# Two fused transformer blocks on one core: the second block's output projection, norms, router logits and last norm with tokens on the partitions

## The reference

```python
h = layer_norm(x) * (1 + sc_m) + sh_m
mix = hybrid_mixer(h, ...)            # ends with  merged @ w_out   (1024 x 1024)
x = layer_norm(alpha * x + g_m * mix, ln_mix_g, ln_mix_b)
h = layer_norm(x) * (1 + sc_f) + sh_f
ffn = grouped_moe(h, ...)             # h @ w_router, top 2 of 16 experts, experts, weighted sum
x = layer_norm(alpha * x + g_f * ffn, ln_ffn_g, ln_ffn_b)
```

## Time and profile before

| what | us |
|---|---|
| median of 3 runs (lowest, highest) | 3239.55 (3237.9, 3245.01) |
| the profiled execution | 3237.79 |
| its span, first to last instruction | 3236.2 |
| PE busy | 3033.9 (94%) |
| DVE, ACT, POOL busy | 1716.0, 1269.9, 1094.5 |
| mean granted clock of PE | 0.978 of full speed |

### The profile page before, as it was taken

How to read it: one execution, slowest core, us unless ns; L and a number is a source line. 1 busy time by engine, 2 the same in 40 slices (tenths; PEclk the granted TensorE clock), 3 DMA queues, 4 the chain that set the end, 5 groups by cost and what they waited for, 6 DMA issues and landing times.

```text
span 3236.2 us, 36830 instructions
## 1 busy us (share of the span) xinstructions
PE 3033.9 (94%) x13878; PEld 2283.3 (71%) x13878; DVE 1716.0 (53%) x2829; ACT 1269.9 (39%) x1901; POOL 1094.5 (34%) x538
## 2 busy tenths in 40 slices
PE   5999999999989999999998999989999986999996
PEld 2666777888756677788885777877777854667664
DVE  5687663212258868322214654647774156666664
ACT  4454434223345453422324444223343223455552
POOL 1242344444324324444443554434444411000001
PEclk9999999999999999999998999999999998999998
DMA  5112563433321146374332335444342315999993
GB/s 223 57 55 72 178 201 114 141 123 103 96 85 59 59 143 221 122 288 137 97 111 77 121 114 176 122 123 115 114 111 72 120 30 201 352 376 385 390 387 126
DMA packets 192665, 501.25 MB, mean 155 GB/s; under 512 B 20144, under 2 KB 102192, under 8 KB 176384
## 3 DMA queue, kind: packets, MB, share of 16 engines
q1 hardware_dynamic: 168816, 415.15, 37.8%
q0 software_dynamic: 13200, 49.32, 4.0%
q10 hardware_dynamic: 10496, 34.71, 3.2%
HBM read 463.83 MB, written 35.29 MB: 154 GB/s over the span
## 4 chain that ended last, share of the span: by engine, by line
PE 75%; DVE 13%; DMA 4%; ACT 4%; issue 3%; ACTq 1%; POOL 1%; DVEq 0%; SPq 0%; POOLq 0%
PE banks L710 19%; PE banks L711 18%; PE banks L712 18%; PE banks L1348 4%; PE banks L1328 2%; PE banks L1330 2%; PE banks L1329 2%; DMA ring<-in_w_all 2%; PE banks L803 1%; PE banks L824 1%; PE banks L770 1%; PE banks L813 1%; DVE abuf L2193 1%; ACT w_hi L1461 1%; DMA routed<-arena 1%
## 5 line engine op out<-in xcount | busy, mean ns | idle before, releaser
L2838 POOL TENSOR_TENSOR w_lo<-ring,w_hi 128x1024 fp32r<-128x1024 f32 (+1 forms) x379 | 917.9, 2424 | 1393.4 <-ACT w_hi L1461 1393.3
L711 PE MATMUL banks<-h_lo,w_hi 128*128 128x512 f32 x2104 | 830.1, 395 | 0.0
L710 PE MATMUL banks<-hx_hi,w_hi 128*128 128x512 f32 (+2 forms) x1400 | 593.7, 424 | 29.8 <-DVE h_lo L2054 9.8
L1461 ACT ACTIVATE w_hi<-ring 128x1024 fp32r<-128x1024 f32 (+1 forms) x379 | 392.8, 1038 | 568.1 <-DMA ring<-in_w_all 481.4
L712 PE MATMUL banks<-hx_hi,w_lo 128*128 128x512 f32 (+2 forms) x1400 | 555.4, 397 | 0.0
L711 PEld LDWEIGHTS banks<-h_lo,w_hi 128*128 128x128 f32 x2104 | 400.4, 190 | 87.0 <-issue 10.4
L710 PEld LDWEIGHTS banks<-hx_hi,w_hi 128*128 128x128 f32 (+2 forms) x1400 | 267.8, 191 | 145.6 <-issue 74.6
L712 PEld LDWEIGHTS banks<-hx_hi,w_lo 128*128 128x128 f32 (+2 forms) x1400 | 267.3, 191 | 60.9 <-issue 0.2
L710 PE MATMUL banks<-hf_hi,w_hi 128*128 128x512 f32 x704 | 275.1, 391 | 4.0 <-DVE h_lo L2054 4.0
L712 PE MATMUL banks<-hf_hi,w_lo 128*128 128x512 f32 x704 | 274.4, 390 | 0.0
L2362 DVE TENSOR_TENSOR arena<-sgs,banks 128x512 f32<-128x512 f32 x44 | 30.3, 689 | 327.3 <-PE banks L712 327.3
(11 more groups left out here) (421 smaller groups left out, 5355.2 us busy)
## 6 DMA issues: line engine op xcount, KB each, us to landing
ring<-in_w_all SPq DMA_DIRECT2D x356, 512.0 KB, 3.8
arena<-in_w_all SPq DMA_DIRECT2D x26, 2048.0 KB, 11.5
arena<-in_w_all SPq DMA_DIRECT2D x96, 512.0 KB, 4.8
ring<-in_w_all SPq DMA_DIRECT2D x46, 1024.0 KB, 6.3
arena<-in_w_all SPq DMA_DIRECT2D x25, 1024.0 KB, 8.1
h<-in_w_all SPq DMA_DIRECT2D x23, 1024.0 KB, 7.9
abuf<-in_w_all SPq DMA_DIRECT2D x32, 512.0 KB, 5.2
routed<-abuf POOLq DMA_DIRECT2D x1, 12288.0 KB, 52.1
```

The costliest lines, as they stand in the source:

```text
L710: pe.matmul(bank[0:m, :], upper, hi, start=first, stop=False)
L711: pe.matmul(bank[0:m, :], upper, lo, start=False, stop=False)
L1461: act.activation(w_hi[s][:, 0:n], raw_w[s][:, 0:n], ACT.Copy).then_inc(w_upper, 1)
L2838: pool.tensor_tensor(w_lo[s][:, 0:n], raw_w[s][:, 0:n], w_hi[s][:, 0:n], ALU.subtract)\
```

## The change

**Out stage.** The tile of an output is now 128 tokens x 512 features: `merged` is stationary, the weights are moving. The order is written by hand: (tokens, features) = (0,0) (1,0) (0,1) (1,1) (2,0) (2,1) (3,0) (3,1). All 8 units of weights stay until the end, so the last four lie beside the ring, over `yT`; they are loaded when `ssdout` has ended. A unit is now one run of 4 KB for each partition, where it was 8 runs of 512 bytes.

```diff
+OUT = [(0, 0), (1, 0), (0, 1), (1, 1), (2, 0), (2, 1), (3, 0), (3, 1)]
+BESIDE_RING = SECOND.at("out", "unit", 4)
-            self.columns(p("out", t), s, 512, t % 4 * P)
+            self.unit(p("out", 6 + t // 4), whole(s, t % 4 * UNIT))
...
-                    if n >= SLOTS:
+                    if n >= BESIDE_RING:
+                        produced(sp, SECOND.at("out", "lin") - 1)
+                        sp.wait_ge(w_in[n % SLOTS], STREAM.units[n - SLOTS][3])
+                    elif n >= SLOTS:
```

```diff
+            def spread_row(columns, pair):
+                for k in range(KC):
+                    mm = pe.matmul(pair[k // 4][:, k % 4 * P:(k % 4 + 1) * P], columns[:, k:k + 1].broadcast_to([P, P]), ident,
+                                   start=True, stop=True)
...
+                if t == 0:
+                    spread_row(v2("ln_mix_g", 0, KC), sc_b)
+                    spread_row(v2("ln_mix_b", 0, KC), pt_b)
+                elif t == 3:
+                    pe.wait_ge(sem("rows_kept"), 2)
+                    spread_row(mod[:, 16:24], sc_b)
...
+            out_chunks(0, range(0, 6), True)
+            out_chunks(1, range(0, 6))
+            out_chunks(0, range(6, KC), True)
+            out_chunks(1, range(6, KC))
...
+            turn_x(0)
+            turn_x(1)
+            out_chunks(2, range(KC))
+            turn_x(2)
+            out_chunks(3, range(KC))
+            turn_x(3)
+            out_chunks(4, range(KC))
+            turn_token_normal(0)
+            out_chunks(5, range(KC))
+            logits(0)
+            turn_token_normal(1)
+            out_chunks(6, range(KC))
+            logits(1)
+            turn_token_normal(2)
+            out_chunks(7, range(KC))
+            logits(2)
+            keep_going(6)
+            turn_token_normal(3)
+            keep_going(2)
+            logits(3)
```

```diff
-            for t in range(8):
-                taken(act, at("out", "lin", t))
-                upper_to(at("out", "unit", t) + 3)
-            layer_norm("ln2", 1, x, v2_at("ln_mix_g"), v2_at("ln_mix_b"), sem("x_affine"))
-            layer_norm("ln3", 2, h, gain_at(8), mod_at(24), sem("h_ready"))
+            upper_to(at("out", "unit") + 3)
+            def scale_x(t):
+                for half in range(2):
+                    act.wait_ge(sem("x_turned"), 2 * t + half + 1)
+                    act.activation(x_tok[:, t, half * SEQ:(half + 1) * SEQ], (sc_b, pt_b)[t % 2][half], ACT.Copy, scale=ALPHA)\
+                        .then_inc(sem("x_scaled"), 1)
...
+            scale_x(0)
+            scale_x(1)
+            upper_to(at("out", "unit") + 7)
+            scale_x(2)
+            token_normal(0)
+            scale_x(3)
+            token_normal(1)
+            hT_made(0)
+            hT_made(1)
+            token_normal(2)
+            hT_made(2)
+            token_normal(3)
+            log_and_exp()
+            hT_made(3, 1)
```

```diff
+            def mixed(n):
+                (t, c), p = OUT[n], at("out", "lin", n)
+                cols = slice(c * SEQ, (c + 1) * SEQ)
                 produced(dve, p)
+                TT(sg[n % 2], lin[p % 2], gate_row[:, cols], MUL).then_inc(lin_free[p % 2], 1)
                 taken(dve, p)
+                dve.wait_ge(sem("x_scaled"), 2 * t + c + 1)
+                mine(TT(x_tok[:, t, cols], x_tok[:, t, cols], sg[n % 2], ADD))
+                mine(dve.bn_stats(stats(t, c), x_tok[:, t, cols]))
...
+            def token_norms(t):
+                moments_known(t)
+                mine(STT(x_tok[:, t, :], x_tok[:, t, :], mean(t), g_row, SUB, MUL))
+                inverted(t, 2 * t)
+                mine(STT(x_tok[:, t, :], x_tok[:, t, :], root_of(t), b_row, MUL, ADD))
+                for c in range(2):
+                    mine(dve.bn_stats(stats(t, c), x_tok[:, t, c * SEQ:(c + 1) * SEQ]))
+                moments_known(t)
+                shifted(t, 2 * t + 1)
```

```diff
-                dve.tensor_copy(yb[par][:, SEQ:], sc_b[1]).then_inc(sem("yd2_done"), 1)
+                TT(yb[par][:, 0:SEQ], sc_b[0], made_row[:, 0:SEQ], MUL)
+                TT(yb[par][:, SEQ:], sc_b[1], made_row[:, SEQ:], MUL).then_inc(sem("yd2_done"), 1)
```

```diff
+                dve.wait_ge(sem("gathered%d" % t), 16)
+                mine(STT(x_tok[:, t, :], htok[:, t, :], weight1[:, t:t + 1], x_tok[:, t, :], MUL, ADD))
+                if t:
+                    shifted(t - 1, 2 * QT + t - 1)
                 dve.wait_ge(sem("paired%d" % t), 16)
+                mine(STT(x_tok[:, t, :], second[:, t, :], weight2[:, t:t + 1], x_tok[:, t, :], MUL, ADD))
+                for c in range(2):
+                    mine(dve.bn_stats(stats(t, c), x_tok[:, t, c * SEQ:(c + 1) * SEQ]))
+                moments_known(t)
...
             for t in range(QT):
+                deviation(t, 2 * QT + t)
+                if t:
+                    y_made(t - 1)
+                normalise(t, QT + t, x_tok[:, t, :])
+            y_made(QT - 1, 1)
```

More of the change, by code:

```diff
@@ L680, in _ @@
             down_in(N_BLK - 1, 0, N_BLK - 1)
+            for t in range(QT):
+                sp.wait_ge(sem("y_done"), 2 * t + 2)
+                sp.dma_start(out[:, :, t * P:(t + 1) * P], x[:, :, t * P:(t + 1) * P]).then_inc(out_done, 16)
+            sp.wait_ge(out_done, 16 * QT)
         @block.tensor
@@ L1266, in _, with out_chunks @@
-            mm.then_inc(aux_full, 1)
-            router_told(pe, "logits_out")
-            aux_for(a + 1)
-            for t in range(QT):
-                mm = pe.transpose(aux[:, t * E_N:(t + 1) * E_N], chosenT[0:E_N, t * P:(t + 1) * P], ident[0:E_N, 0:E_N])
-            mm.then_inc(aux_full, 1)
+            def out_chunks(n, ks, merged_ready=False):
+                (t, c), p = OUT[n], at("out", "lin", n)
+                bank, tokens = lin[p % 2], slice(t * P, (t + 1) * P)
+                if ks[0] == 0:
+                    bank_for(p)
+                for k in ks:
+                    u = at("out", "unit", 4 * c + k // 2)
+                    if merged_ready:
+                        pe.wait_ge(sem("m_split"), LAYERS * KC + k + 1)
+                    pe.wait_ge(w_lower, STREAM.units[u][4])
+                    cols = slice(k % 2 * SEQ, (k % 2 + 1) * SEQ)
+                    upper, lower = hi_at(u)[:, cols], lo_at(u)[:, cols]
+                    pe.matmul(bank, mg2_hi[:, k, tokens], upper, start=(k == 0), stop=False)
+                    pe.matmul(bank, mg2_hi[:, k, tokens], lower, start=False, stop=False)
+                    mm = pe.matmul(bank, mg2_lo[:, k, tokens], upper, start=False, stop=(k == KC - 1))
+                if ks[-1] == KC - 1:
+                    mm.then_inc(lin_full[p % 2], 1)
@@ L1279, in _ @@
                     for k in range(4):
-                        mm = pe.transpose(bank[:, k * P:(k + 1) * P], h[:, 4 * half + k, t * P:(t + 1) * P], ident)
+                        mm = pe.transpose(bank[:, k * P:(k + 1) * P], hT[:, 4 * half + k, t * P:(t + 1) * P], ident)
                     mm.then_inc(sem("ht_done"), 1)
+            for n in range(2):
+                taken(pe, SECOND.end["lin"] - 2 + n)
+            spread_row(mod[:, 40:48], lin)
             router_told(pe, "chosen")
-            aux_for(a + 2)
+            aux_for(a + 1)
             for t in range(QT):
@@ L1351, in down_block @@
                 mm.then_inc(sem("d_done"), 1)
-            for n in range(2):
-                taken(pe, SECOND.end["lin"] - 2 + n)
             pe.wait_ge(sem("htok_done"), 2 * QT)
+            pe.wait_ge(sem("rows_kept"), 4)
             first_rows()
@@ L1906, in _, with keep_row @@
                     spread_rows(i + 1)
+            def keep_row(n, row, pair):
+                act.wait_ge(sem("rows_spread"), n + 1)
+                for half in range(2):
+                    ins = act.activation(row[:, half * SEQ:(half + 1) * SEQ], pair[half], ACT.Copy)
+                ins.then_inc(sem("rows_kept"), 1)
             for t in range(8):
@@ new lines, in hT_made @@
+            def hT_made(t, halves=2):
+                for half in range(halves):
+                    turned_half(t, half, gain_at(8), mod_at(24), sem("hT_done"))
+            scale_x(0)
[11 more added lines that the diff above has]
+            log_and_exp()
@@ L1971, in _, with step @@
             upper_weights(1, (2, 3))
-            def step(b, par, first=False):
+            def step(b):
                 act.wait_ge(sem("hidden"), b)
@@ new lines, in _, with turned_half @@
+            dve.wait_ge(sem("rows_kept"), 3)
+            mixed(0)
+            mixed(1)
+            mixed(2)
+            token_norms(0)
+            mixed(3)
+            token_norms(1)
+            mixed(4)
+            mixed(5)
+            token_norms(2)
+            mixed(6)
+            mixed(7)
+            token_norms(3)
+            def turned_half(i, scale, shift, signal):
+                t = i % QT
+                dve.wait_ge(sem("normal_turned"), 2 * i + 2)
+                for k in range(4):
```

(2 more changed lines are left out.)

235 lines of the change are left out of this document (121 added, 114 removed).

## The result

| | before | changed |
|---|---|---|
| median, us (lowest to highest, 4 runs each) | 3238.73 (3233.21 to 3245.01) | 3199.76 (3198.31 to 3203.63) |
| the profiled execution | 3237.79 | 3199.39 |
| its span | 3236.2 | 3197.8 |
| mean granted clock of PE | 0.978 | 0.979 |

What follows compares the result with a forecast made beforehand. PE was taken as full in the expert loop and out stage, leaving two serial norm pieces, before the router and at the end. Terms +2.1 - 22.9 - 16.5 = -37.3 us gave a 3202 us median, range 3189 to 3217.

Steps and rivals of the forecast that it cites:

- `ssdout`: Three spreads of 8 products on PE: the first two cost nothing under PE's wait for DVE, the third +2.1 us.
- up to 2 back: In turn 0 of ssdout, more PE work in the gap can give back up to 2 us; taken as 0.
- The stall at (0,1): Out stage: PE waits for POOL's lower parts, which start after ACT's scalings; 8.7 us that nothing hides.
- The out stage's second half: From 2613 PE's work sums to 34.6 us, last product at 2647.6, router at 2661.3 against 2684.2: -22.9 us.
- hidden, except for the last: Out stage: four tiles ask 39.6 us of DVE against PE's pace of 13 each, so only the last tile's norm shows.
- no idle time of DVE between the tiles of the out stage: Out stage sign: the prediction is wrong if DVE has no idle time between the tiles.
- Experts: Expert loop: DVE makes both halves of `yb`, +0.7 us a block, at cost 0; 16 us if DVE set the pace.
- The end: After the last expert block: DVE's groups of 4.5 us, then ACT, turns and store, ending at 3219.7 against 3236.2: -16.5 us.
- (a): Out stage and end: DVE becomes the bound, with `bn_stats` at 1.21 and small tiles at 0.6; 3215 us, chance 0.20.
- (b): Product (0,1) stalls less because POOL or ACT gets on earlier, and ssdout's clock stays up; 3191 us, chance 0.10.
- (c): Norms not overlapped at all, each tile's norm going round PE, ACT and DVE in line; 30 us back, 3232, chance 0.05.
- (d): Out stage: bursts between waits for POOL keep PE's clock low until the router; 47 us, time 3249, chance 0.03.

Runs made afterwards that it cites:

- the reordered kernel: Changed kernel with ACT's upper parts before scalings, evacuations split around roots, last norm's pass earlier, half of group 2's tiles on DVE: 3195.25 us, again 3191.23.

## Why the prediction was right, and where it was not

**`ssdout`: right.** The third spread cost 18.14 - 16.32 = 1.8 us where 2.1 was taken, and the first two nothing. That turn 0 even got 1.95 shorter was named as possible ("up to 2 back") and costed at 0; the profiles show both outcomes.

**The stall at (0,1): right.** Forecast: the product ends at 2613, 26.6 us after the mark, held by POOL's lower parts that start only after ACT's scalings. Measured: DVE takes it 27.38 after the mark, POOL's four parts stand back to back in 9.7 us, PE waits 4.7 and 0.6 us for them. Taking the cause away gave 7.8 back (8.7 forecast). Missed was a smaller wait of 1.2 us on a unit of the ring: POOL made two lower parts in a row, in 5.2 us, and the second came late.

**The out stage's second half: mis-sized by 4.5 us.** The step that failed is "hidden, except for the last". It compared 39.6 us of DVE for four tiles with 13 of PE for each, as if DVE's work were spread evenly. But the order gives DVE a whole norm behind (0,1) and another behind (1,1), and a `mixed` with a norm took 7.87 us where PE needs 5.44 for a product and 0.87 to 1.7 for turns. That alone did no harm, since the reordered kernel has it too.

What reached PE was the order of ACT's stream: tile 0's eight small tiles stand behind tile 1's norm, so the first logits waited 0.84 us for them. Then the clock fell, and PE needed 1.6 us more up to the second logits. With ACT's order changed, DVE's work the same and no wait of PE, the second half took 35.2 us, 0.6 more than the 34.6 forecast, most of it the logits (1.7 each, 1.5 taken). So 2.7 of the 3.3 us lost between (0,1) and the last product are ACT's order with the fall of the clock behind it, which doesn't come in every profile. ACT's order also made DVE wait 2.54 for a root, but PE had no wait for that.

One of the prediction's own signs of being wrong, no idle time of DVE between the tiles of the out stage, is there for three products: beside two waits of 0.33 us for a root, DVE works through from 2610.10 to 2627.98. The last product came 65.3 after the mark, not 61.2; 0.8 of that was already there at (0,1). The steps behind it were near: 14.05 to the copy where 13.7 were summed, with `bn_stats` 0.69 (0.6 taken), eight small tiles 2.90, so 0.36 each (0.3), and logits 1.7 to 2.0 (1.5). The 5.5 us for `token_norms` were right (2650.21 to 2655.75), but not as added up: the terms given there come to 5.1.

**Experts: right.** DVE's second half of `yb` stayed hidden at 99 of 100; only the profile says so, no variant changed it alone.

**The end: mis-sized by 2.6 us.** From the first gathered rows to the end it took 32.8 us (3164.99 to 3197.8), where 29.9 was summed. The sum let DVE's groups of 4.5 us set the pace and added ACT's eight tiles once, at 2.4. A group took DVE 4.97, and from the second on ACT's stream of 8 tiles (2.90), a wait for PE's turns (1.13) and the pass (1.14) was slower still, 5.2 a group: its last pass ended 25.4 after the first rows, not 22.3. Against that the store landed early. Its issue and landing were costed at 4.7, and 3.95 passed from DVE's last tiles to the end; the DMA rows of the end give

```profile
out<-x SPq DMA_DIRECT2D x4, 512.0 KB, 3.5
```

3.5 us for the stores in runs of 512 bytes, not the 4.3 of the earlier trace rows. Here the rule of the Trainium skill (DMA: Bandwidth & Descriptors, Specifications), weighed in the prediction and not taken, gave the better number.

**The rivals.** (a) DVE as bound was not what happened: `bn_stats` took 0.69 and not 1.21, and of the 3.3 us that the second half lost (37.9 from (0,1) to the last product, 34.6 forecast) none was left to DVE's amount of work once ACT's order was changed. (b) named the stall's size, which was right as it stood, and a clock that stays up in turn 0, which it did here. (c) was priced at 30, and the kernel that builds it lost 24.9, with a low clock and misplaced fillers in it. (d) did not come in the changed kernel, with the clock back at 1.00 after 2605 and one short fall from 2632; the experiment with the norms after all products shows that the mechanism is real once PE has nothing between the bursts.

**The total.** The errors of +4.5 and +2.6 were met by -2.0 in turn 0, -3.6 ahead of `ssdout` and -2.4 in router and experts. Of these the 3.6 is scatter, the 2.0 comes in half of the executions profiled, and whether the 2.4 is real is open. That the sum came within 2 us is luck in part. The changed kernel's other median, 3207.77 on another chip, also lies in the range; with the measured sizes of the three terms the forecast would have been 3202 + 4.5 + 2.6 - 0.3 = 3209.

## What to carry to other kernels

When work is moved under a stage that PE fills, lay the covering and the covered engine side by side product by product, in the order of their streams: an average over the stage hides the stretch where the other engine has a norm and a tile between two products, and a third engine between the two (here ACT) can turn a delay with room into a wait. In an in-order stream, work that another engine waits for (the upper parts of the next weights, a root of one column) goes ahead of work that nobody awaits yet; here such swaps, with half of a group's tiles given to DVE, were worth 13.8 us by the marks. And judge a change of a few us by marks in the profile on both sides of it, since the rest of the kernel scatters by more than that.

## What was unexpected of the hardware

- From the mark to the copy the same code mostly repeats within 0.1 us (68.88 and 68.84, 79.36, 79.27 and 79.28, 97.79 and 97.83; the one exception is 79.89), while the last lower parts of `yT` begin anywhere within 12 us between executions of code that is the same up to there but for merged semaphores.
- Turn 0 takes 13.5 or 15.15 us in the same code, with PE's granted clock at 1.00 throughout or with a dip to 0.5 for one or two stretches of 2.5 us. What decides between them was not found.
- A wait of PE of 0.83 to 0.86 us, ahead of logits and turns, was followed by 2.5 us or more at the lower level in four of five profiles of the same code, and in the fifth the clock stayed at 1.00. One profile with a filler in its place kept 1.00 too, which therefore proves little.
- `bn_stats` over 128 x 512 takes 0.69 us, as a tensor-tensor pass of that size, and the aggregate 0.21. Eight products with 16 columns take 1.7 to 2.0 us at full clock and 3.60 at the lower level, hardly less than eight with 128 columns (2.07).
